# A scan branch's norm factor applied behind its projection, with its mean between the products of a gate group

## The reference, cut to what matters

```python
h = rmsnorm(x, attn_norm_g[layer])
proj = h @ w_in[layer]
gm_u, gm_v, ssm_z, ssm_xbc, ssm_dt, da_q, da_k, da_v, gates = split_cols(proj, IN_SIZES)
y_a = chunked_spatial_gating(...)
y_b = mamba2_mixer(ssm_z, ssm_xbc, ...)        # ends in: rmsnorm(y * silu(z), norm_g), 1024 wide
y_c = diff_attention(da_q, da_k, da_v, ...)
g = sigmoid(gates).reshape(bsz, s, 3, D_MODEL)
merged = g[:, :, 0] * (y_a @ w_branch_a) + g[:, :, 1] * (y_b @ w_branch_b) + g[:, :, 2] * (y_c @ w_branch_c)
x = x + merged @ w_out[layer]
```

## Time and profile before

| | |
|---|---|
| median of 3 runs | 1901.75 us (1900.01 to 1902.54) |
| profiled execution, its own time | 1899.97 us |
| its span | 1898.2 us |
| PE busy | 1875.0 us, 99% of the span |
| DVE busy | 1277.6 us, 67% |
| ACT busy | 1029.5 us, 54% |
| chain that ended last | PE 90%, DVE 6%, DVEq 2%, ACT, DMA and issue 1% each |
| mean granted clock of PE | 0.995 of full |

### The profile page before, as it was taken

The page is one execution under the profiler, slowest core; times in us unless marked ns, Lnnn a source line. Parts: engine busy times, 40 slices in busy tenths (PEclk is TensorE's granted clock), DMA queues, the critical chain, the costliest instruction groups (busy, mean ns, idle before and its releaser), DMA issues.

```text
span 1898.2 us, 28721 instructions
## 1 busy us (share of the span) xinstructions
PE 1875.0 (99%) x11910; PEld 1694.9 (89%) x11910; DVE 1277.6 (67%) x1728; ACT 1029.5 (54%) x1147; POOL 0.4 (0%) x6
## 2 busy tenths in 40 slices
PE   7999999999999999999999999999999999999998
PEld 7898789998999878899889988899988988889997
DVE  6867777986686867798664455677655455568654
ACT  5656645655564664465544456455544456555543
POOL 0000000000000000000000000000000000000000
PEclk9999999999999999999999999999999999999999
DMA  8665655655866665655555566465556466545553
GB/s 216 185 146 134 171 181 184 197 179 186 168 156 156 147 147 177 200 180 185 184 188 182 169 178 204 155 201 178 178 181 200 149 200 190 166 161 178 184 186 100
DMA packets 241473, 332.35 MB, mean 175 GB/s; under 512 B 8072, under 2 KB 153748, under 8 KB 241344
## 3 DMA queue, kind: packets, MB, share of 16 engines
q1 hardware_dynamic: 241224, 330.43, 58.6%
q10 hardware_dynamic: 120, 0.09, 0.0%
HBM read 329.43 MB, written 1.07 MB: 174 GB/s over the span
## 4 chain that ended last, share of the span: by engine, by line
PE 90%; DVE 6%; DVEq 2%; ACT 1%; DMA 1%; issue 1%; SPq 0%
PE psum L542 36%; PE psum L554 14%; PE psum L556 14%; PE psum L555 14%; PE psum L626 3%; DVE w_low L369 1%; DVEq L1318 1%; PE psum L869 1%; PE psum L889 1%; PE psum L713 1%; DMA w_raw<-in_w_in 1%; DVE w_low L370 1%; PE psum L658 1%; DVE act_lo L1386 1%; PE psum L877 1%
## 5 line engine op out<-in xcount | busy, mean ns | idle before, releaser
L377 ACT ACTIVATE w_hi<-w_raw 128x2048 fp32r<-128x2048 f32 (+2 forms) x312 | 579.1, 1857 | 324.3 <-PE psum L556 274.4
L369 DVE TENSOR_TENSOR w_low<-w_raw,w_hi 128x1024 fp32r<-128x1024 f32 (+1 forms) x312 | 375.2, 1203 | 358.0 <-ACT w_hi L377 349.7
L542 PE MATMUL psum<-act_hi,w_hi 128*128 128x256 f32 x2016 | 574.5, 285 | 1.6 <-DVE w_low L369 1.1
L542 PE MATMUL psum<-act_lo,w_hi 128*128 128x256 f32 x2016 | 571.8, 284 | 0.0
L542 PE MATMUL psum<-act_hi,w_low 128*128 128x256 f32 x2016 | 571.8, 284 | 0.0
L554 PE MATMUL psum<-w_hi,act_hi 128*128 128x512 f32 x1280 | 509.3, 398 | 0.0
L556 PE MATMUL psum<-w_hi,act_lo 128*128 128x512 f32 x1280 | 500.4, 391 | 0.0
L555 PE MATMUL psum<-w_low,act_hi 128*128 128x512 f32 x1280 | 500.4, 391 | 0.0
L542 PEld LDWEIGHTS psum<-act_hi,w_hi 128*128 128x128 f32 x2016 | 387.1, 192 | 3.4 <-DVE w_low L369 1.5
L542 PEld LDWEIGHTS psum<-act_lo,w_hi 128*128 128x128 f32 x2016 | 387.3, 192 | 0.2
L542 PEld LDWEIGHTS psum<-act_hi,w_low 128*128 128x128 f32 x2016 | 387.2, 192 | 0.0
(11 more groups left out here) (218 smaller groups left out, 1358.8 us busy)
## 6 DMA issues: line engine op xcount, KB each, us to landing
w_raw<-in_w_in SPq DMA_DIRECT2D x124, 1024.0 KB, 5.9
w_raw<-in_ffn_w_up SPq DMA_DIRECT2D x40, 1024.0 KB, 5.1
w_raw<-in_w_up SPq DMA_DIRECT2D x40, 1024.0 KB, 5.1
w_raw<-in_ffn_w_down SPq DMA_DIRECT2D x16, 1024.0 KB, 5.1
w_raw<-in_w_down SPq DMA_DIRECT2D x16, 1024.0 KB, 5.1
w_raw<-in_w_branch_b SPq DMA_DIRECT2D x8, 1024.0 KB, 5.1
w_raw<-in_w_out SPq DMA_DIRECT2D x8, 1024.0 KB, 5.0
w_raw<-in_w_a SPq DMA_DIRECT2D x8, 1024.0 KB, 5.0
```

The lines of the kernel that those rows point to most:

```text
L369: dve.tensor_tensor(lo[:, 0:cut, :], of[:, 0:cut, :], hi[:, 0:cut, :], ALU.subtract).then_inc(w_lo_front, 1)
L377: act.activation(group_view(whi, q % HIGH, g), group_view(raw, q % LOW, g), ACT.Copy).then_inc(w_hi, 1)
L542: last = mm(o, held, moved, start=start and k == ks[0] and m == 0, stop=stop and k == ks[-1] and m == 2, skip_group_check=shared)
```

## The change

- PE: `scan_mean` is cut into eight pieces of two matmuls. `wide_products` calls one behind the three products of each k tile of GA1. The spread of the factor behind GA2 goes.
- ACT: the root moves from behind GA1 to behind BA1, ahead of the root of the attention branch. y is rounded behind GA1 in eight instructions that multiply by the gain alone (`yb_high`), in place of one behind GA3.
- DVE: the reciprocal moves behind BA1 (`yb_rstd`). `yb_norm` goes; `yb_low` behind GA2 makes `act_lo` from y, gain and `act_hi` at once, in eight instructions, and the pass behind GA3 goes.
- DVE's `gated` multiplies the four tiles of BB by `y_rstd` too (one SCALAR_TENSOR_TENSOR in place of a TENSOR_TENSOR).

```diff
-            def wide_products(g, q, t, ks):
+            def wide_products(g, q, t, ks, between=None):
...
                     last = mm(o, xl, hi[:, k, :], start=False, stop=g["closes"] > 0 and k == g["kt"] - 1)
+                    if between is not None:
+                        between(4 * t + k)
...
-            def scan_mean(i):
-
-                pe.wait_ge(step("yb_sq"), i + 1)
-                for tt in range(TT):
-                    for k in range(KD):
-                        last = mm(pC[:, S + tt:S + tt + 1], sq8[:, k, tt * P:(tt + 1) * P], ones[:, 0:1], start=k == 0, stop=k == KD - 1)
-                last.then_inc(step("yb_ms"), 1)
+            def scan_mean(i, at):
+
+                if at == 0:
+                    pe.wait_ge(step("yb_sq"), i + 1)
+                for tt, k in ((at // 4, 2 * at % 8), (at // 4, 2 * at % 8 + 1)):
+                    last = mm(pC[:, S + tt:S + tt + 1], sq8[:, k, tt * P:(tt + 1) * P], ones[:, 0:1], start=k == 0, stop=k == KD - 1)
+                if at == 7:
+                    last.then_inc(step("yb_ms"), 1)
...
+                              (lambda at: scan_mean(i, at)) if G[n]["name"] == "GA1" else None)
...
-                    GU1=lambda: gate_mix(i), GA1=lambda: scan_mean(i),
-                    GA2=lambda: (spread("yb_rstd", i + 1, yrstd, "yb_spread"), attn_turn(i)), GA3=lambda: attn_scores(i, 0), GB1=lambda: attn_wturn(i, 0),
+                    GU1=lambda: gate_mix(i), GA2=lambda: attn_turn(i), GA3=lambda: attn_scores(i, 0), GB1=lambda: attn_wturn(i, 0),
...
+                def yb_high():
+                    for k in range(KD):
+                        last = A(ahi[:, A_YB + k, :], xbc[:, k, :], ACT.Copy, scale=col(1, "sg", k))
+                    last.then_inc(step("yb_hi"), 1)
...
-                    GA1=lambda: root("yb_ms", i + 1, pC[:, S:S + TT], yrstd, "yb_root"),
-                    GA3=lambda: (split_high(i, "yb32_ready", i + 1, slice(A_YB, A_YB + 8), xbc[:, 0:8, :], "yb_hi"), attn_exp(0)), GB3=lambda: attn_exp(1), BA0=o_square,
-                    BA1=lambda: small_root(i, "o_sums", os_, P, "o_root"))
+                    GA1=yb_high, GA3=lambda: attn_exp(0), GB3=lambda: attn_exp(1), BA0=o_square,
+                    BA1=lambda: (root("yb_ms", i + 1, pC[:, S:S + TT], yrstd, "yb_root"), small_root(i, "o_sums", os_, P, "o_root")))
...
-                    TTo(v, wide, v, ALU.mult).then_inc(taken["dve"], 1)
+                    if factor is None:
+                        TTo(v, wide, v, ALU.mult).then_inc(taken["dve"], 1)
+                    else:
+                        STT(v, wide, factor[:, t:t + 1], v, ALU.mult, ALU.mult).then_inc(taken["dve"], 1)
...
-                def yb_norm():
-                    dve.wait_ge(step("yb_spread"), i + 1)
+                def yb_low():
+                    dve.wait_ge(step("yb_hi"), i + 1)
                     for k in range(KD):
-                        last = STT(xbc[:, k, :], xbc[:, k, :], col(1, "sg", k), spread_rstd, ALU.mult, ALU.mult)
-                    last.then_inc(step("yb32_ready"), 1)
+                        last = STT(alo[:, A_YB + k, :], xbc[:, k, :], col(1, "sg", k), ahi[:, A_YB + k, :].bitcast(f32), ALU.mult, ALU.subtract)
+                    last.then_inc(step("yb_ready"), 1)
+
+                def yb_rstd():
+                    dve.wait_ge(step("yb_root"), i + 1)
+                    V.reciprocal(yrstd[:, :], yrstd[:, :])
...
-                    GA1=lambda: rstd_of("yb_root", i + 1, yrstd, "yb_rstd"), GA2=yb_norm,
-                    GA3=lambda: (split_low("yb_hi", i + 1, slice(A_YB, A_YB + 8), xbc[:, 0:8, :], "yb_ready"), attn_weights(0)), BA0=o_sums, BA1=o_norm)
+                    GA2=yb_low, GA3=lambda: attn_weights(0), BA0=o_sums, BA1=lambda: (yb_rstd(), o_norm()))
```

More of the change, by code:

```diff
@@ L566, in merged_turn, with proj_wide @@
                 last.then_inc(step("mg_turned"), 1)
-            def proj_wide(b, i, n, G, normed=None):
+            def proj_wide(b, i, n, G, normed=None, between=None):
                 g = G[n]
@@ L587, in proj_wide @@
                     else:
-                        last = wide_products(g, at_group(b, i, n), t, range(g["kt"]))
+                        last = wide_products(g, at_group(b, i, n), t, range(g["kt"]), between)
                     if t == 0 and g["closes"]:
@@ L810, in stream @@
                 if G[n]["form"] == "W":
-                    proj_wide(b, i, n, G, norm_count(b, i, 0, 0) if G[n]["name"] in ("PU2", "PU3") else None)
+                    proj_wide(b, i, n, G, norm_count(b, i, 0, 0) if G[n]["name"] in ("PU2", "PU3") else None,
+                              (lambda at: scan_mean(i, at)) if G[n]["name"] == "GA1" else None)
                 elif G[n]["name"] in firsts:
@@ L1423, in tile_arrived, with gated @@
                     arrived(b, i, n)
-            def gated(b, i, n, g, gate, into, whole):
+            def gated(b, i, n, g, gate, into, whole, factor=None):
                 for t in range(TT):
@@ L1695, in take @@
                         gates, whole = dict(BA=(G0, "first"), BB=(ug[:, :, :], "more"), BC=(SZ, "last"))[kind]
-                        gated(1, i, n, g, lambda t: by_token(gates)[:, t, g["c0"]:g["c0"] + 512], by_token(G0), whole)
+                        gated(1, i, n, g, lambda t: by_token(gates)[:, t, g["c0"]:g["c0"] + 512], by_token(G0), whole,
+                              yrstd if kind == "BB" else None)
                     elif kind in ("OUT", "DN"):
```

## The result

| | median | ratio to before (95% interval) |
|---|---|---|
| before, runs beside the changed kernel | 1900.43 us (1900.01 to 1902.54) | |
| changed kernel | 1889.88 us (1889.63 to 1892.41) | 0.9944 (0.9930 to 0.9959) |

The forecast was 1893.8, in a range from 1890.8 to 1898.8. The interval of the ratio ends at 0.9959, so the gain is clear of the noise. The profiled execution took 1889.88 us, its span went from 1898.2 to 1888.1.

A forecast was written before the change was run, and what follows sets the result against it. PE, busy 1875.0 of 1898.2 us, was taken to set the time. GA1 to the turn 3.8, attention chain 2.6 and second fall 1.6 sum to 8.0 us, from 1901.75 to 1893.8; range 1890.8 to 1898.8.

The forecast's parts named there:

- the base: Whole kernel: 1901.75 us, taken as start of the sum because the profiled execution (1899.97) lay 1.8 us under the median.
- the price of a piece: PE in GA1: four passes of 0.109 us plus a 0.09 us restart, eight times, 4.2 us; 1.9 us saved per layer.
- layer 1's wait behind GB1: PE's wait for the attention weights in layer 1: falls from 2.17 to about 0.9 us, 1.3 us gained.
- The clock: PE in GA1 and GA2: the fall to half clock behind the mean block goes, granted clock 1.00 in both layers.
- the 1.69 us behind the block: PE behind the mean block: extra time of slow products at half clock, counted as gained in each layer.
- No new waits: PE in GA1 and the turn of q and k: yb_sq has 1.4 us to spare, the rope 1.2 us.
- The copies on ACT: Eight scaled copies of y on ACT behind GA1: 3.8 us, hidden with 1.4 us to spare.
- The attention chain: From the turn of q and k to the weights behind GB1: 1.25 us sooner in layer 0, 1.3 in layer 1.
- The second fall: Layer 1 behind the wait after GB1: 3.4 us at half clock goes with the shorter wait, 1.6 us gained.
- The first: Rival: the attention chain doesn't shorten, only 3.8 us come, perhaps the second fall stays; 1897.9 us; 12%.
- the third: Rival: switches drain the array, a piece costs 0.83 us, and the clock falls through GA1; 1908 us; 3%.
- the second: Rival: the clock falls anyway in or behind GA1, and layer 1's later fall stays; 1898.6 us; 10%.

The follow-up runs named there:

- e4: Changed kernel with the mean in two blocks of eight matmuls, one behind each token tile of GA1; 1891.03 us, ratio 0.9958.
- e5: Changed kernel with the mean in one block behind GA1, each mean matmul moving 128 columns of ones instead of one; 1890.74 us, ratio 0.9949.
- e10: The changed kernel run once more, unedited; 1890.32 us, ratio 0.9945 to the kernel before.
- e1: Kernel before with only the mean cut into eight pieces between GA1's products; spread, norm and both passes over y stay; 1900.05 us, ratio 1.0002.
- e2: Changed kernel with the mean in one block of one-column matmuls behind GA1 again; 1895.81 us, ratio 0.9976.
- e9: Changed kernel with one extra 128x2048 pass (2.3 us) on DVE ahead of the attention weights; 1896.25 us, ratio 0.9977.
- e3: Changed kernel with both steps on y (yb_high, yb_low) behind GA3 again; 1891.94 us, ratio 0.9961.

## Why the prediction was right and where it was off

The forecast was 3.9 us above the measured 1889.88. The steps that failed are terms of the sum: the base 1.8 us, the price of a piece 1.0, layer 1's wait behind GB1 0.3, and a fall that was not in it, 0.7 (the last 0.1 is in the rest of the program). The mechanisms came as forecast, one of them in part by luck. For the price of a piece one row more is needed, the weight loads of the first piece:

```profile
164.73 0.64 PEld L668 LDWEIGHTS psum<-ones,tmp 128*128 128x128 f32 x4
```

- **The base.** This is the largest miss and the one that put the time out of the range. I added 1.78 us, from the profiled execution's 1899.97 to the median of three runs, 1901.75, and took the 8.0 from there. That median didn't last: with two more runs it was 1900.43, and in the three later groups 1900.2 to 1900.5. On its own profiled execution the sum gave 1892.0, and the range would have begun at 1889.0.
- **The price of a piece** was mis-sized: 0.53 us forecast, 0.46 measured. The restart of 0.09 was right (165.64 - 165.31 = 0.33 for a product of 0.23, so 0.10). Wrong was to charge each piece four passes of 0.109 = 0.44: they take 165.31 - 164.95 = 0.36. Its first weight load starts at 164.73 us, under the product that began at 164.72, and the four passes take little more than the time of three. So what a further block costs in restart it nearly saves in its first pass. e4 and e5 agree: A is 14.61, 14.58 and 14.47 us with eight, two and one blocks. 3.8 us were forecast for both layers, 4.7 measured.
- **What was not in the sum:** layer 1's fall behind dt_proj, 1.5 us less 0.8 for the wait that took its place. The edit didn't touch it, and in e10 the fall was there: this gain of 0.7 us is luck. Without it the time is still below the range, as e10's 1890.32 is.
- **The range.** Its lower end had room for pieces without a restart and for both waits gone, 3 us in all; of these 1.3 came. It had none for a wrong base or for a fall missing elsewhere, 2.5 us together.
- **The clock.** Right: behind the block it fell, with the pieces it stays up (e1, e2), and e5 shows that it was the one column of each matmul, not the length or the place of the block. The Trainium skill's rule that the prediction weighed (page "TensorE: Matmul & The Clock Gate", section "HAM oscillation — how this bites in real kernels"), loss of clock by idle gaps, does not cover this: PE was busy without a gap in e2's block too, 3.50 of 3.50 us, and the clock fell. A fall behind a wait is seen as well (e9, layer 1), but not behind each.
- **The slow stretch alone.** The prediction took the 1.69 us behind the block as gained once the clock stays up. That held only because the spread went in the same change: e1 shows that DVE's row of work up to `y_rstd` ended no sooner. The sum is right for the whole change; nothing in it said that its halves don't add.
- **No new waits** on `yb_sq` or the rope: right. The copies on ACT were cheaper than taken, 3.29 us for 3.8.
- **The attention chain.** Right in layer 0 to 0.02 us (1.25 forecast, 1.27), 0.3 short in layer 1: in the kernel before the same chain was 0.36 us longer there (B of 21.75 against 21.39), and in the changed kernel it isn't. Of the two ways in which the chain was to get shorter, the pass of 2.29 us that leaves DVE is the one that counts; e9 shows it by putting one back, and e3 that the stage played no part. The exponentials came 0.35 us sooner as forecast, but in e9, which keeps this, layer 0's B is that of before.
- **The second fall.** It went, 1.6 us as forecast, but the reason given was weak: the waits of 1.79 and 2.17 us were taken as the two sides of a line. e1 has 2.17 without a fall and e9 1.85 with one. That the wait of 0.6 us is safe is seen fourteen times, not proven; and that the kernel before had the fall in the profiled execution is in part luck.
- **The rivals.** None came. The first (chain not shortened) is refuted by B, the third (drained switches) by the pieces' 0.46 us, and the second by the clock at the mean in all ten profiles with pieces or wide columns.

## What to carry to other kernels

A block of very narrow matmuls can cost twice: its weight loads, and the slow products behind it (in all four profiled stretches behind the mean's block, and in 18 of 20 behind dt_proj's). Either spread it between products or make its columns wide; widening was free here, where 32 passes took 3.49 us with 1 column and with 128. Before taking a slow stretch away, ask which chain on another engine it covers, and read that chain to its end: e1 gained nothing, since DVE reached the reciprocal at the same 16.22 us. And a median of three runs is no better a base than the profiled execution if single runs scatter by 5 us and more.

## What the runs showed of the hardware that was not expected

- 32 passes with weight loads of 128x128 and one column each take 3.49 us, and with 128 columns each the same 3.49 us. PE is busy in both; behind the first the clock is granted at half (1.2 GHz) for 3.4 or 6.8 us (before, e2), behind the second at full (e5).
- Changing between plain float32 matmuls and fp32r products 16 times instead of twice in a group costs 0.14 us in all (A of the changed kernel against e5, whose one block takes the 3.49 us of before).
- The two halves of this change were worth 0 and 4.4 us alone, and 10.5 together.
